# Expert rows moved in transfers of 64 lanes, with a reordered last routing tile, in a one-layer hybrid mixer and mixture-of-experts kernel

## What is computed

```python
def hierarchical_moe(xn, ...):                       # t = xn, 512 x 1024
    group_probs = softmax(t @ w_router_group)        # 4 groups
    g_idx = argmax(group_probs)
    in_group = (t @ w_router_expert)[g_idx]          # 8 experts of that group
    top_p, top_i = top_k(softmax(in_group), 2)       # two experts a token
    combine = one_hot(g_idx * 8 + top_i) * p_group * top_p / sum(top_p)
    for e in range(32):
        hid = silu(t @ w_expert_gate[e]) * (t @ w_expert_up[e])      # 1024 x 256 each
        out = out + combine[:, e:e + 1] * (hid @ w_expert_down[e])   # 256 x 1024
x = x + hybrid_mixer(rms_norm(x));  x = x + hierarchical_moe(rms_norm(x));  return rms_norm(x)
```

## Time and profile before

| | us |
|---|---|
| runs shown | 713.92, 714.67, 717.95 (median 714.67) |
| the profiled execution's own time | 714.88 |
| its span, first to last instruction | 712.9 |
| TensorE busy (97% of the span) | 690.4 |
| VectorE busy | 372.7 |
| ScalarE busy | 254.7 |
| POOL busy | 80.0 |

### The profile page before, as it was taken

The page is one execution under the profiler, slowest core; times in us unless marked ns, Lnnn a source line. Parts: engine busy times, 40 slices in busy tenths (PEclk is TensorE's granted clock), DMA queues, the critical chain, the costliest instruction groups (busy, mean ns, idle before and its releaser), DMA issues.

```text
span 712.9 us, 10002 instructions
## 1 busy us (share of the span) xinstructions
PE 690.4 (97%) x3923; PEld 507.5 (71%) x3923; DVE 372.7 (52%) x725; ACT 254.7 (36%) x423; POOL 80.0 (11%) x116
## 2 busy tenths in 40 slices
PE   7999999999999999999999999999999999999794
PEld 6888988777777777788888888665555556555442
DVE  5378996667676868656446214852423221212227
ACT  7332134577676777544243211210111111111113
POOL 2000922000000101100003000011111112121000
PEclk9999999999999999999999999999999999999998
DMA  7523144322222111493406699699999999999983
GB/s 241 176 63 116 61 126 147 134 74 75 74 74 68 46 60 53 161 384 114 135 2 236 239 376 348 268 353 394 399 417 421 403 420 419 418 418 418 420 353 130
DMA packets 60360, 164.57 MB, mean 231 GB/s; under 512 B 7866, under 2 KB 39687, under 8 KB 47892
## 3 DMA queue, kind: packets, MB, share of 16 engines
q1 hardware_dynamic: 54820, 151.77, 56.1%
q0 software_dynamic: 5488, 12.11, 4.5%
HBM read 155.68 MB, written 16.00 MB: 241 GB/s over the span
## 4 chain that ended last, share of the span: by engine, by line
PE 90%; DMA 4%; DVE 4%; ACT 1%; issue 1%; SPq 0%; POOLq 0%; DVEq 0%; ACTq 0%
PE psum L1731 31%; PE psum L2155 15%; PE psum L1830 12%; PE psum L2181 8%; PE psum L2008 6%; PE psum L1842 3%; PE psum L2121 2%; DMA ring_e<-y_dram 2%; DVE ring_e L1093 2%; PE psum L1855 1%; PE psum L1884 1%; DMA y_dram<-ye,slots 1%; PE psum L2164 1%; PE psum L1967 1%; PE psum L1919 1%; PE psum L1907 1%
## 5 line engine op out<-in xcount | busy, mean ns | idle before, releaser
L1731 PE MATMUL psum<-xh,wh 128*128 128x512 f32 x256 | 99.9, 390 | 0.8 <-DVE xl L1093 0.8
L1731 PE MATMUL psum<-xl,wh 128*128 128x512 f32 x256 | 99.6, 389 | 0.0
L1731 PE MATMUL psum<-xh,wl 128*128 128x512 f32 x256 | 99.6, 389 | 0.0
L1096 DVE TENSOR_TENSOR wl<-raw,wh 128x1280 fp32r<-128x1280 f32 (+4 forms) x37 | 71.8, 1946 | 24.8 <-ACT wh L789 9.0
L1093 DVE SCALAR_TENSOR_TENSOR hid<-psum,rslot,act_g 128x256 f32<-128x256 f32 x17 | 8.2, 484 | 95.1 <-PE psum L2155 94.6
L1731 PEld LDWEIGHTS psum<-xh,wh 128*128 128x128 f32 x256 | 48.1, 188 | 11.1 <-DVE xl L1093 1.0
L1731 PEld LDWEIGHTS psum<-xh,wl 128*128 128x128 f32 x256 | 48.1, 188 | 9.9
L1731 PEld LDWEIGHTS psum<-xl,wh 128*128 128x128 f32 x256 | 48.1, 188 | 9.8
L1830 PE MATMUL psum<-xh,wh 128*128 128x512 f32 x128 | 51.3, 401 | 1.3 <-DVE k_fl L1093 1.3
L1830 PE MATMUL psum<-xh,wl 128*128 128x512 f32 x128 | 50.1, 391 | 0.0
L1830 PE MATMUL psum<-xl,wh 128*128 128x512 f32 x128 | 49.9, 390 | 0.0
(11 more groups left out here) (383 smaller groups left out, 1517.1 us busy)
## 6 DMA issues: line engine op xcount, KB each, us to landing
raw<-in_w_gate SPq DMA_DIRECT2D x16, 1024.0 KB, 6.4
raw<-in_w_in SPq DMA_DIRECT2D x9, 1024.0 KB, 5.5
ring_w<-in_w_expert_gate SPq DMA_DIRECT2D x8, 1024.0 KB, 20.4
ring_w<-in_w_expert_up SPq DMA_DIRECT2D x8, 1024.0 KB, 17.1
ring_h<-in_w_expert_down SPq DMA_DIRECT2D x8, 1024.0 KB
ring_h<-in_w_expert_gate SPq DMA_DIRECT2D x6, 1024.0 KB
ring_e<-in_w_expert_down SPq DMA_DIRECT2D x6, 1024.0 KB, 17.7
ring_e<-in_w_expert_gate SPq DMA_DIRECT2D x6, 1024.0 KB, 22.5
```

What stands on the lines that cost most here:

```text
L1096: return dve.tensor_tensor(dst, src, hi.bitcast(F32), ALU.subtract)
L1731: last = nc.tensor.matmul(dst, a, b, start=start and n == 0, stop=stop and n == len(seq) - 1)
```

## The change

- POOL issues a gather and a scatter for each expert of a turn, of 64 lanes each, where there was one of 128. The second has its row numbers in new columns `slots_b` and `toks_b`, in partitions 0 to 63. Turn 8 keeps one of each. VectorE fills the new columns at the first table, in the exchange of turn 2 and in `overflow_column`. The counts awaited on `g_full` and `scattered` follow (`HALVES`, `one_less`).
- `slot_no` numbers the lanes in another order.
- The read-back of a token tile is one transfer of 8 KB rows.
- TensorE waits for `fk` after 24 matmuls of `x_products()`, not ahead of them.
- The last residual, its transposes, ScalarE's copies and its logits go in two halves; `route` makes two of its steps earlier; `rv` of the last two tiles and the subtraction into `rg` come later; `choose_rows(0, 1)` comes behind the last logits.
- ScalarE copies both banks into `xg`; the first table's products come behind the first transposes of `xg`.

```diff
+        def blocks_of(n):
+
+            return (slice(0, KC // 4), slice(KC // 4, KC // 2)) if n == 2 * NT - 1 else (slice(0, KC // 2),)
...
+        def one_less(s, i=PART):
+
+            return 16 if s == PART % 2 and i >= PART else 0
...
-                sp_e.wait_ge(S["x2_ready"], NT + t + 1)
+                sp_e.wait_ge(S["x2_ready"], NT + t + 1 if t < NT - 1 else 2 * NT + 1)
...
                 for t in tiles:
-                    for j in range(2):
-                        sp_e.dma_start(yt[t][:, j, :], y_v[t, :, j, :]).then_inc(y_in[t], 16)
+                    sp_e.dma_start(yt[t], y_v[t]).then_inc(y_in[t], 16)
...
             for s in range(2):
-                sp_e.wait_ge(scattered[s], 16 * (NPAIR // 2 - s))
+                sp_e.wait_ge(scattered[s], HALVES * (NPAIR // 2 - s) - one_less(s))
...
-                        base, step = SLOT // 2 * a + 8 * d, 1
-                        if d % 2:
+                    for k, d in enumerate((2, 0, 1, 3) if a else (0, 2, 3, 1)):
+                        base, step = SLOT // 2 * a + 8 * k, 1
+                        if k % 2:
                             base, step = base + 7, -1
...
             def gather(c, i, s):
 
-                n, p = rows_of(c, i), column(c, i)
-                pool.indirect_dma_start(out=xg[n, s, :], out_offset=None, in_=x2_dram[:, :],
-                                        in_offset=bass.IndirectOffsetOnAxis(ap=toks[n, p], axis=0),
+                p = column(c, i)
+                pool.indirect_dma_start(out=xg[first, s, :], out_offset=None, in_=x2_dram[:, :],
+                                        in_offset=bass.IndirectOffsetOnAxis(ap=toks[first, p], axis=0),
                                         bounds_check=last_token, oob_is_err=False).then_inc(g_full[s], 16)
+                if whole(c, i):
+                    pool.indirect_dma_start(out=xg[second, s, :], out_offset=None, in_=x2_dram[:, :],
+                                            in_offset=bass.IndirectOffsetOnAxis(ap=toks_b[first, p], axis=0),
+                                            bounds_check=last_token, oob_is_err=False).then_inc(g_full[s], 16)
 
             def scatter(c, i, s):
 
-                n, p = rows_of(c, i), column(c, i)
-                pool.indirect_dma_start(out=y_dram[:, :], out_offset=bass.IndirectOffsetOnAxis(ap=slots[n, p], axis=0),
-                                        in_=ye[n, :], in_offset=None, bounds_check=last_row,
+                p = column(c, i)
+                pool.indirect_dma_start(out=y_dram[:, :], out_offset=bass.IndirectOffsetOnAxis(ap=slots[first, p], axis=0),
+                                        in_=ye[first, :], in_offset=None, bounds_check=last_row,
                                         oob_is_err=False).then_inc(scattered[s], 16)
+                if whole(c, i):
+                    pool.indirect_dma_start(out=y_dram[:, :], out_offset=bass.IndirectOffsetOnAxis(ap=slots_b[first, p], axis=0),
+                                            in_=ye[second, :], in_offset=None, bounds_check=last_row,
+                                            oob_is_err=False).then_inc(scattered[s], 16)
...
                 b, t = n // NT, n % NT
-                act.wait_ge(S["xt2_ps"], n + 1)
-                act.activation(xt2[:, t % 2, b * (KC // 2):(b + 1) * (KC // 2), :], bank[4 + n % 2][:, :].rearrange("p (c s) -> p c s", s=P),
-                               ACT.Copy).then_inc(S["moved_a"], 1)
+                for k, part in enumerate(blocks_of(n)):
+                    act.wait_ge(S["xt2_ps"], n + k + 1)
+                    act.activation(xt2[:, t % 2, b * (KC // 2):(b + 1) * (KC // 2), :][:, part, :],
+                                   bank[4 + (n + k) % 2][:, :].rearrange("p (c s) -> p c s", s=P)[:, part, :], ACT.Copy).then_inc(S["moved_a"], 1)
...
+            for b in range(2):
+                act.wait_ge(S["routed_ps"], NT + b + 1)
+                act.activation(xg[:, 0, b * T:(b + 1) * T], bank[b][:, :], ACT.Copy).then_inc(S["moved_a"], 1)
             act.wait_ge(S["sq2_sum"], 1)
             act.activation(stat[:, 1, :], stat[:, 0, :], ACT.Sqrt, bias=eps[:, 0:1], scale=1.0 / D).then_inc(S["root"], 1)
 
-            act.wait_ge(S["routed_ps"], NT + 1)
-            act.activation(xg[:, 0, 0:T], bank[0][:, :], ACT.Copy).then_inc(S["moved_a"], 1)
...
                 dve.wait_ge(S["out_ps"], b * NT + t + 1)
-                half = x2[:, t, b * T:(b + 1) * T]
-                dve.tensor_tensor(half, half, bank[t][:, :], ALU.add).then_inc(S["x2_ready"], 1)
+                for part in (slice(0, T // 2), slice(T // 2, T)) if b and t == NT - 1 else (slice(0, T),):
+                    half = x2[:, t, b * T:(b + 1) * T][:, part]
+                    dve.tensor_tensor(half, half, bank[t][:, part], ALU.add).then_inc(S["x2_ready"], 1)
...
+                st.link(dve.reduce_max(rs[:, 3, t:t + 1], re[:, 2, :], AX.X))
+                st.link(stt(re[:, 3, :], re[:, 2, :], rs[:, 3, t:t + 1], from_last[:, 0:NE], ALU.is_equal, ALU.mult))
                 yield
-                first_max(re[:, 2, :], NE, rs[:, 3, t:t + 1], re[:, 3, :], best)
-                st.mark(dve.tensor_scalar(rg[:, 0, t, :], gl, top, None, ALU.subtract))
+                st.link(dve.reduce_max(best, re[:, 3, :], AX.X))
                 dve.wait_ge(S["m_ready"], 2 * t)
                 stt(rmask[:, t, :], re[:, 3, :], best, ro[:, 0, t, :], ALU.is_equal, ALU.add).then_inc(S["m_ready"], 1)
                 dve.tensor_scalar(ro[:, 1, t, :], re[:, 3, :], best, None, ALU.is_equal).then_inc(S["m_ready"], 1)
+                if t < NT - 2:
+                    row_values(t)
+                yield
+
+            def row_values(t):
...
                     next(routes[t - 1])
             choose(NT - 2)
-            dve.wait_ge(S["sq_done"], 3 * NT)
-            dve.reduce_sum(stat[:, 0, :], sq_part[:, :, :], AX.X).then_inc(S["sq2_sum"], 1)
             for part in range(2):
                 next(routes[NT - 1])
             choose(NT - 1)
+            for t in (NT - 2, NT - 1):
+                row_values(t)
             rank_tokens(NT - 2)
             rank_tokens(NT - 1)
-            dve.wait_ge(S["routed_ps"], NT + 2)
-            dve.tensor_copy(xg[:, 0, T:2 * T], bank[1][:, :]).then_inc(S["hot_ready"], 1)
+            dve.wait_ge(S["sq_done"], 3 * NT)
+            dve.reduce_sum(stat[:, 0, :], sq_part[:, :, :], AX.X).then_inc(S["sq2_sum"], 1)
 
             def slot_columns(n, found):
...
                     dve.tensor_scalar(slots[half, 0:NPAIR], table[half, h, :], float(UNUSED), None, ALU.add).then_inc(S["slots_in"], 1)
+                dve.tensor_scalar(slots_b[0:SLOT, 0:NPAIR], table[0:SLOT, 1, :], float(UNUSED), None, ALU.add).then_inc(S["slots_in"], 1)
                 dve.wait_ge(S["slots_in"], n)
                 dve.tensor_scalar(toks[:, 0:NPAIR], slots[:, 0:NPAIR], 1, None, ALU.arith_shift_right).then_inc(S["idx_ready"], 1)
+                dve.tensor_scalar(toks_b[0:SLOT, 0:NPAIR], slots_b[0:SLOT, 0:NPAIR], 1, None, ALU.arith_shift_right).then_inc(S["idx_ready"], 1)
...
+                st.link(dve.tensor_copy(slot_f[first, :], slots_b[first, 0:NPAIR]))
+                exchanged(moved[first, :], slot_f[first, :], slot_f[first, OVER:OVER + 1], gap[first, :])
+                st.link(dve.tensor_copy(slots_b[first, FIXED:NPAIR], slot_f[first, FIXED:NPAIR]))
+                st.mark(dve.tensor_scalar(toks_b[first, FIXED:NPAIR], slots_b[first, FIXED:NPAIR], 1, None, ALU.arith_shift_right))
...
-            for name in ("sq", "sk", "sv", "fq", "fk", "fv"):
+            for name in ("sq", "sk", "sv", "fq", "fv"):
                 evacuated(pe, name)
...
 
-            gates(PER_TILE)
+            gates(BEHIND_SCORES)
+            evacuated(pe, "fk")
...
-                for c in range(KC // 2):
-                    d = (b * (KC // 2) + c) * P
-                    last = nc.tensor.transpose(bank[4 + n % 2][:, c * P:(c + 1) * P], x2[:, t, d:d + P], ident[:, :])
-                last.then_inc(S["xt2_ps"], 1)
+                for k, part in enumerate(blocks_of(n)):
+                    if k:
+                        pe.wait_ge(S["x2_ready"], n + k + 1)
+                        pe.wait_ge(S["moved_a"], n)
+                    for c in range(KC // 2)[part]:
+                        d = (b * (KC // 2) + c) * P
+                        last = nc.tensor.transpose(bank[4 + (n + k) % 2][:, c * P:(c + 1) * P], x2[:, t, d:d + P], ident[:, :])
+                    last.then_inc(S["xt2_ps"], 1)
...
@@ -2015,9 +2061,9 @@
 
             choose_rows(0, 0)
             router_transposes(2 * NT - 1)
-            choose_rows(0, 1)
             rank_products(NT - 2)
             router_logits(2 * NT - 1)
+            choose_rows(0, 1)
...
-
-            first_table()
...
-                    pe.wait_ge(S["moved_a"], 2 * NT + 1)
-                    pe.wait_ge(S["hot_ready"], ALL_HITS + 1)
+                    pe.wait_ge(S["moved_a"], 2 * NT + 3)
...
```

(7 more changed lines are left out.)

55 lines of the change are left out of this document (31 added, 24 removed).

## The result

| | before | changed |
|---|---|---|
| median of 4 runs, us | 715.28 | 722.99 (722.71 to 723.04) |
| ratio, 95% interval | 1 | 1.0102 (1.0072 to 1.0133) |
| span of the profiled execution, us | 712.9 | 721.0 |

The change costs 7.7 us, 1.0%. The prediction, 710.5 us with a range to 713.6, was wrong in size and sign.

A forecast was written before the change was run, and what follows sets the result against it. TensorE was busy 97%, with the end set by the stream of transfers. Terms of -3.1, -1.4, +0.3, 0 and -0.1 made -4.3 us, 714.88 to 710.6; against the median it predicted 710.5 us, range 708.3 to 713.6.

The forecast's parts named there:

- Term 1: One gather and scatter per expert on POOL evens rows over the engines: -3.1 us; the added transfers cost 0.
- Term 2: TensorE's wait for fk's projection, moved behind 24 matmuls: -1.4 us.
- Term 3: The last token tile's routing: first expert product later, +0.3 us, bounds -0.2 and +0.7.
- Term 4: Work added to VectorE in turn 2's exchange: TensorE stands 0.7 us, taken by slack in the weight wait; net 0.
- Term 5: Read-back of token tiles in 8 KB rows: -0.1 us.
- Rival d: POOL's queue, with four transfers a turn, becomes the bound: slower, 718.8 us; chance 0.06.
- Rival a: The transfer engines' lag is their own, so term 1 is worth 1 us or less: 712.7 us; chance 0.17.
- Rival b: The 1.4 us of term 2 are lost in the score steps, which VectorE starts late: 711.9 us; chance 0.12.
- c: All of the transfer engines' skew goes, term 1 being 4.3 to 5.0 us: 709 us; chance 0.10.

The follow-up runs named there:

- a1: The changed kernel with one 128-lane gather a turn again, the scatters still split; 711.08 us, ratio 0.9952 to the kernel before.
- a3: The changed kernel with gathers and scatters both of 128 lanes again; 713.15 us, ratio 0.9977 to the kernel before.
- b1: The changed kernel with 128-lane gathers interleaving both experts, scatters split, and slots numbered even and odd; 711.33 us, ratio 0.9941 to before.
- b4: The kernel before with only the wait for fk's projection moved behind 24 gate products; 712.70 us, ratio 0.9975 to before.
- a2: The changed kernel with one 128-lane scatter a turn again, the gathers still split; 725.13 us, ratio 1.0148 to the kernel before.

## Why the prediction was wrong

*Term 1, the rows, had the wrong sign.* Its first half was right. The half that was late is that of the fuller experts; even rows made the engines end together (5.0 us unused became 2.3); the rows of a 64-lane transfer are spread over all engines, as assumed. (The recorded 145 and about 98 rows are 143 and 100 to 106 when each turn's gather and scatter are counted, which makes the estimate of 3.9 us 3.6.) The step that failed is the cost: "What it adds on POOL: ... Cost 0". It looked at the issue times, the landings and the reuse of `ye`, and not at what the transfers in flight do to the rest of the traffic. The sentence that allowed it, that the turn-8 scatter was the only 64-lane transfer to look at, was false. Put in its place: 15 split gathers make all packets slower for 3 to 7 us each, 16.1 - 3.6 = 12.5 us per engine. Less 1.5 that the stream starts earlier and 2.7 that end together, that is 8.3 us, against 8.1 in the span.

The 3.1 us for balance alone may have been a little high. `a1`, with two thirds of the skew left, gained 2.1 us over `a3`, and `b1`, with none, 2.6 by the ratios, give or take 1.2. Two thirds of the skew could stay for nearly the whole gain: as soon as weights come before TensorE wants them, the rest is worth little. The prediction had asked whether TensorE could use the 3.1 us, and answered from the waits of the last two turns alone.

*Term 2, the wait for `fk`, was right.* The first gate product starts at 137.41 and the first score product at 144.34, where it was at 145.90; the ratio of the kernel with this edit alone is 1.8 us (0.8 to 2.8), against 1.4 forecast and 1.56 in the trace:

```profile
137.41 0.40 PE L1869 MATMUL psum<-xh,wh 128*128 128x512 f32 x1
...
144.34 0.32 PE L1925 MATMUL psum<-q_s,k_s 64*128 64x128 f32 x1
```

*Term 3, the last tile, was +0.1 us instead of +0.3.* The first expert product comes 1.45 us earlier, of which 1.56 are `fk`'s:

```profile
461.64 1.16 PE L2164 MATMUL psum<-ident,xg 128*128 128x128 f32 x8 [0.69 <-ACT xg L1039]
...
463.71 2.59 PE L2200 MATMUL psum<-ring_z,xT 128*64 128x256 f32 x22
```

The transposes wait for ScalarE until 461.64, and the table's products then run within the wait for `xT`. That is the case which the prediction had as its lower bound, -0.2.

*Term 4, VectorE in turn 2, was right.* TensorE stands 0.60 us for `hid` there (0.7 forecast), and it was free only because weights came last:

```profile
503.50 0.50 PE L2209 MATMUL psum<-ident,hid 128*128 128x128 f32 x2 [0.60 <-DVE hid L1115]
```

*Term 5* can't be seen. `a3`, which holds terms 2 to 5, is 0.4 us slower than `b4` with term 2 alone, in sets on different chips, less than these runs tell apart.

*The rivals.* Rival d named the right side by the wrong mechanism. The queue isn't the bound: each half of a scatter lands sooner than a whole one did (8.5 us), not after 12.

```profile
y_dram<-ye,slots POOLq DMA_INDIRECT x15, 6.6
y_dram<-ye,slots_b POOLq DMA_INDIRECT x14, 7.3
```

`a1` and `a2`, with 45 and 46 transfers and 14 us between them, exclude it. Rival a, that the lag is the engines' own, holds for about 3 us of the 9. Rival b didn't occur: the first score product kept its 1.56 us. Nor did c: 2.3 of the 5.0 us stayed unused. No case in the list was "the new transfers slow the packets of the others"; the trace had it.

## What to carry to other kernels

Where a stream of transfers is the bound, judge an added or reshaped transfer by what it does to the bytes per second of the others, not by its own landing: the busy share stayed at 1.02 while the rate fell from 414 to 370 GB/s, so read both columns. If a trace already has one transfer of the new shape in each direction, look at each of them; here the one that read 64 partitions was harmless and the one that wrote them was not. Rows that lie on a few engines can be spread by renumbering lanes inside a 128-lane transfer, and evening them is worth only as much as the waits that they cause.
